# Forty of the first token block's expert sums moved from VectorE to GpSimd in a decoder layer kernel

## What is computed

```python
def peer_ffn(x, w_query, sub_keys, expert_u, expert_v):
    ...
    experts = jnp.take_along_axis(cand_idx..., top_pos, axis=-1)   # 128 experts for each token
    gate = jax.nn.softmax(top_s, axis=-1)
    def one_block(args):
        xb, eb, gb = args
        h = jax.nn.gelu(jnp.einsum('td,ted->te', xb, expert_u[eb]), approximate=False)
        return jnp.einsum('te,ted->td', gb * h, expert_v[eb])
    ...
h = layer_norm(ALPHA * h + ff, ln3_g[l], ln3_b[l])
```

## Time and profile before

| | us |
|---|---|
| median of 3 runs | 3145.84 |
| lowest and highest of them | 3145.17, 3148.16 |
| the profiled execution's own time | 3145.48 |
| its span | 3143.6 |

### The profile page before, as it was taken

How to read it: one execution, slowest core, us unless ns; L and a number is a source line. 1 busy time by engine, 2 the same in 40 slices (tenths; PEclk the granted TensorE clock), 3 DMA queues, 4 the chain that set the end, 5 groups by cost and what they waited for, 6 DMA issues and landing times. The chain is left out here.

```text
span 3143.6 us, 37681 instructions
## 1 busy us (share of the span) xinstructions
PE 2694.7 (86%) x16328; PEld 2218.2 (71%) x16328; DVE 1272.7 (40%) x1693; ACT 426.7 (14%) x916; POOL 803.9 (26%) x536
## 2 busy tenths in 40 slices
PE   8899999998999999999898986788766767676566
PEld 7898899998889899889898885788422223222222
DVE  0122001010100155734443455447677775655654
ACT  1121100021000111111101210101100001211121
POOL 0000000000000011212211232233466565555652
PEclk9999999999999999999999988899888888888899
DMA  8976378776837799998998989999999999999996
GB/s 326 305 267 227 136 296 298 285 296 228 311 138 287 260 363 385 354 369 344 424 424 357 383 321 423 420 396 425 409 421 422 421 421 421 421 422 421 422 422 280
DMA packets 126932, 1096.41 MB, mean 349 GB/s; under 512 B 13440, under 2 KB 22064, under 8 KB 28080
## 3 DMA queue, kind: packets, MB, share of 16 engines
q1 hardware_dynamic: 50512, 542.08, 44.3%
q0 software_dynamic: 76256, 551.94, 42.9%
HBM read 1084.52 MB, written 9.44 MB: 348 GB/s over the span
## 5 line engine op out<-in xcount | busy, mean ns | idle before, releaser
L601 PE MATMUL PS<-arena 128*128 128x128 f32 (+1 forms) x13952 | 1883.7, 297 | 78.4 <-DMA arena<-units 64.5
L601 PEld LDWEIGHTS PS<-arena 128*128 128x128 f32 x13952 | 1798.6, 194 | 158.5 <-DMA arena<-units 57.7
L949 PE MATMUL PS<-arena 128*128 128x512 f32 x1152 | 628.6, 706 | 275.8 <-DMA arena<-peer_v,arena 264.2
L949 PEld LDWEIGHTS PS<-arena 128*128 128x128 f32 x1152 | 254.1, 228 | 649.3 <-issue 591.8
L1382 DVE CUSTOM_DVE_ANT_0 arena<-arena 128x2048 f32<-128x2048 f32 x256 | 586.8, 2292 | 287.5 <-DMA arena<-peer_u,arena 281.0
L566 POOL DMA_INDIRECT arena<-peer_u,arena x256 | 399.1, 1559 | 892.5 <-DVE arena L1382 678.2
L566 POOL DMA_INDIRECT arena<-peer_v,arena x256 | 393.8, 1538 | 449.3 <-PE PS L949 214.2
L1392 DVE SCALAR_TENSOR_TENSOR arena<-arena 128x2048 f32<-128x2048 f32 x112 | 263.4, 2352 | 132.0 <-DMA arena<-peer_v,arena 128.7
L972 ACT ACTIVATE arena<-PS 128x512 f32<-128x512 f32 (+2 forms) x154 | 84.5, 549 | 1313.5 <-PE PS L601 1199.9
L1347 ACT ACTIVATE arena<-arena 128x128 f32<-128x128 f32 x144 | 57.9, 402 | 722.9 <-PE PS L949 721.5
L537 POOL DMA_DIRECT2D arena<-ln_rows x2 | 1.3, 640 | 384.7 <-DVE arena L1727 384.7
(11 more groups left out here) (186 smaller groups left out, 1049.0 us busy)
## 6 DMA issues: line engine op xcount, KB each, us to landing
arena<-units SPq DMA_DIRECT2D x243, 2048.0 KB, 9.1
arena<-w_ukv SPq DMA_DIRECT2D x16, 512.0 KB, 10.4
arena<-ln_rows SPq DMA_DIRECT2D x6, 1024.0 KB, 14.8
arena<-ln_rows POOLq DMA_DIRECT2D x4, 1024.0 KB, 18.6
arena<-peer_u,arena POOLq DMA_INDIRECT x256, 23.5
arena<-peer_v,arena POOLq DMA_INDIRECT x256, 23.8
rb_scratch<-arena POOLq DMA_DIRECT2D x1, 3072.0 KB, 38.5
arena<-rb_scratch SPq DMA_DIRECT2D x12, 256.0 KB, 9.8
```

The source lines that it names most:

```text
L601: ins = mm(bank[:, first:first + rhs.shape[1]], lhs, rhs, start=k == 0, stop=k == KT - 1)
L949: ins = mm(Y[c], diag[:, n % 4 * P:(n % 4 + 1) * P], rows[b][:, c * 512:(c + 1) * 512], start=n == first_used[tb], stop=False, skip_group_ ...
```

## The change

1. **More V rows early, and spread wider.** `SOON` goes from 28 to 40 and `FIRST` from 72 to 52: from U row 52 to U row 127, 40 V rows stand between them, about one behind every second U row. `LATE` becomes 168, the rest 344 entries.
2. **GpSimd sums them.** A new `add_row` on GpSimd scales the row in place by its gate and adds it to `acc`, two instructions over 128x2048 fp32. It stands in GpSimd's queue behind the fetch of the entry four places later (`LAG` = 4) and waits for its row to land. VectorE's own sums into `acc` wait until all 40 are there.
3. **Turns count dots only.** VectorE's turns hold 3 dots where they held 4 entries (scores aside). The turn in the second norm is gone. All 128 dots are done by the third step of CO.
4. **Gates earlier.** gelu and gates of the first `HALF` slots (40, were 56) are made between the recurrence and the branch gates. ScalarE's `gelu(0)` moves ahead of the gate evacuations.
5. **No identity matmuls.** `LAST` and L956 go; `last_norm` first adds each PSUM bank to VectorE's sums. VectorE and TensorE now alternate up to the last row.
6. In the last part `choose(1, k)` comes every six dots, not eight.

```diff
-HALF = 56
-FIRST = 72
-SOON = (NE - FIRST) // 2
+HALF = 40
+FIRST = 52
+SOON = 40
 GATED = 112
-LAST = 4
+LAG = 4
...
     for e in range(NE):
         order.append(("U", e))
-        if e >= FIRST and (e - FIRST) % 2:
-            order.append(("V", (e - FIRST) // 2))
+        if e >= FIRST and len(order) - e <= (e - FIRST + 1) * SOON // (NE - FIRST):
+            order.append(("V", len(order) - e - 1))
...
+                elif before[1] < SOON:
+                    pool.wait_ge(added, before[1] + 1)
...
-            for kind, s in ARRIVALS:
+            def add_row(s):
+
+                b, nth, _ = ROWS["V", s]
+                if s == 0:
+                    pool.wait_ge(begun, 1)
+                    pool.wait_ge(gated, 1)
+                else:
+                    pool.wait_ge(added, s)
+                pool.wait_ge(row_landed[b], 16 * (nth + 1))
+                nc.gpsimd.tensor_scalar(rows[b], rows[b], gates[0][:, s:s + 1], None, ALU.mult).then_inc(scaled_row, 1)
+                pool.wait_ge(scaled_row, s + 1)
+                nc.gpsimd.tensor_tensor(acc, acc, rows[b], ALU.add).then_inc(added, 1)
+
+            for n, (kind, s) in enumerate(ARRIVALS):
                 gather(kind, s)
+                if n >= LAG and ARRIVALS[n - LAG][0] == "V" and ARRIVALS[n - LAG][1] < SOON:
+                    add_row(ARRIVALS[n - LAG][1])
...
-                if e == NE - LAST:
-
-                    pe.wait_ge(v_summed, summed_to(s))
-                    for c in range(4):
-                        ins = mm(Y[c], ident, sums[tb][:, c * 512:(c + 1) * 512], start=False, stop=False, skip_group_check=True)
-                    ins.then_inc(all_summed, 1)
...
-                end = min(at[0] + n, LATE)
-                for kind, s in ARRIVALS[at[0]:end]:
-                    if kind == "U":
-                        dot(s)
-                    else:
-                        if s == 0:
-                            gate(0)
-                        add_row(s)
+                end = min(at[0] + n, NE)
+                for e in range(at[0], end):
+                    dot(e)
...
                 for s in range(8):
+                    if tb and s == 1:
+                        gate(0)
...
                 second_norm(tb)
-                if tb:
-                    turn(4)
                 choose(tb, 0)
...
-            def last_norm(tb, parts, done):
-
+            def last_norm(tb, banks, done):
+
+                parts = [sums[tb][:, c * 512:(c + 1) * 512] for c in range(4)]
                 for c in range(4):
+                    link(v.tensor_tensor(parts[c], parts[c], banks[c], ALU.add))
                     link(v.bn_stats(stats[:, 48 + 6 * c:54 + 6 * c], parts[c]))
```

More of the change, by code:

```diff
@@ L126, in on_vector @@
     if s < SOON:
-        return True
-    if s % NE >= NE - LAST:
         return False
@@ L138, in used_to @@
 def used_to(s):
-    return s + 1 - summed_to(s)
+    return s + 1 - SOON - summed_to(s)
 def arrivals():
@@ L394, in trunk_layer @@
         dot_done, gelu_done, v_summed, v_used = (sem(n) for n in ("dot_done", "gelu_done", "v_summed", "v_used"))
-        gated, all_summed = sem("gated"), sem("all_summed")
+        gated, begun, scaled_row, added = (sem(n) for n in ("gated", "begun", "scaled_row", "added"))
         gh_done, diag_done = sem("gh_done"), sem("diag_done")
@@ L1252, in trunk @@
                     mean_roots(q)
+                    gelu(0)
                 for j in range(4):
@@ L1269, in trunk @@
                             relu_out(tb, s)
-                if tb:
-                    gelu(0)
                 q_out(tb, 0)
@@ L1390, in add_row @@
                     dve.wait_ge(gh_done, e + 1)
+                elif summed_to(s) == 1:
+                    dve.wait_ge(added, SOON)
                 dve.wait_ge(row_landed[b], 16 * (nth + 1))
@@ L1690, in trunk @@
                 if tb:
-                    turn(4)
+                    turn(3)
                 gated_sums(q)
                 if tb:
-                    turn(4)
+                    turn(3)
                 normed_out(q)
                 if tb:
-                    turn(4)
+                    turn(3)
                 for s in range(8):
+                    if tb and s == 1:
+                        gate(0)
                     if s < 4 * (tb + 1):
@@ L1747, in trunk @@
                 second_norm(tb)
-                if tb:
-                    turn(4)
                 choose(tb, 0)
                 final_rows(tb)
-                link(v.tensor_scalar(sums[tb], h_tok[tb], ALPHA, None, ALU.mult))
+                mark(v.tensor_scalar(sums[tb], h_tok[tb], ALPHA, None, ALU.mult), begun, tb + 1)
             trunk(0)
@@ L1758, in _ @@
             trunk(1)
-            turn(LATE)
+            turn(NE)
             gate(1)
-            def last_norm(tb, parts, done):
+            def last_norm(tb, banks, done):
+                parts = [sums[tb][:, c * 512:(c + 1) * 512] for c in range(4)]
                 for c in range(4):
+                    link(v.tensor_tensor(parts[c], parts[c], banks[c], ALU.add))
                     link(v.bn_stats(stats[:, 48 + 6 * c:54 + 6 * c], parts[c]))
@@ L1780, in _ @@
                     dot(s)
-                    if s % 8 == 1 and s // 8 - NE // 8 < PEER_HEADS - 1:
-                        choose(1, s // 8 - NE // 8 + 1)
+                    k, more = divmod(s - NE, 6)
+                    if more == 1 and k < PEER_HEADS - 1:
+                        choose(1, k + 1)
                 else:
@@ L1786, in _ @@
                     if s == NE + PK:
-                        dve.wait_ge(all_summed, 1)
                         dve.wait_ge(v_used, used_to(NE - 1))
@@ L1791, in _ @@
                         add_row(s)
-            dve.wait_ge(all_summed, 2)
             dve.wait_ge(v_used, used_to(TB * NE - 1))
```

## The result

| | us |
|---|---|
| before, median | 3145.51 |
| after, median (lowest, highest) | 3237.89 (3235.54, 3238.32) |
| ratio, 95% interval | 1.0291, 1.0274 to 1.0309 |
| span of the profiled execution, before and after | 3143.6, 3236.5 |

The change costs 92 us. The forecast was 3151 with a range of 3116 to 3184.

A forecast was written before the change was run, and what follows sets the result against it. Total taken as transfers, which alone set the pace from 2220 us on, plus idle DMA time. 13.1 + 25.4 - 4.7 - 30.0 - 7.5 + 9 = +5.3 us on 3145.5 gave 3151, range 3116 to 3184.

The forecast's parts named there:

- Term 6: GpSimd's own passes over the early V rows: +9 us, from 0 to 39, for VectorE instructions that may find GpSimd at work.
- p: GpSimd's price per early V row, two passes: taken as 7 us, with bounds of 2.35 and 9.4 us.
- The second rival: GpSimd becomes the bound in attention turns and cross-attention heads, deciding from p = 7.3 us: slower, 3181, chance 0.20.
- Terms 1 to 3: Rows moved between stages of the first part: attention +13.1 us, merge to cross-attention +25.4, CO to PQ -4.7.
- Term 1: Attention: 13 more rows cost 32.5 us, less 19.4 us of idle DMA time, +13.1 us.
- the faster rival: The passes get their rows for free, 8.4 us idle at 1650 fills, GpSimd costs nothing: 3129, chance 0.23.
- Term 3: CO to PQ: 13 fewer rows; TensorE can't use the freed transfers, only its wait for the keys goes, -4.7 us.
- The gap: CO to PQ: DMA engines lack 13 rows, 32.5 us, before TensorE's last unit; later rows can't fill it.
- Term 4: Rows-only part: 12 rows fewer at 2.50 us each, -30.0 us.
- Term 5: The end, from the last landing to the last matmul and bank additions: -7.5 us.
- The third rival: GpSimd's first sum waits for late gates of slots 0 to 39, stalling all rows: time near no change, chance 0.04.
- The case at the faster end: The faster rival, 3129, chance 0.23; its floor, with all 25 early rows free, is 3108.

The follow-up runs named there:

- no sums: The changed kernel with GpSimd's two passes over each of the 40 early V rows replaced by one-column writes, sums left out: 3150.84 us, 1.0019 of before.
- four writes: The changed kernel with four GpSimd writes of the landed row's buffer in place of the two passes, sums left out: 3174.06 us, 1.0093.
- the long writes: The changed kernel with five GpSimd writes of the row's buffer and one of 1408 columns in place of the passes, sums left out: 3202.64 us, 1.0187.
- the run with VectorE's sums: The changed kernel with the 40 early sums done by VectorE in its turns, same order of rows: 3160.39 us, 1.0047.
- the new end alone: The kernel before without identity matmuls, V rows alternating up to the last, bank sums added by VectorE: 3139.49 us, 0.9981.
- the faster version: The kernel before with the new end, 34 early V rows instead of 28, summed by VectorE, four entries per attention turn instead of three: 3124.62 us, 0.9937.

## Why the prediction failed, and where it held

**Term 6, GpSimd itself, failed.** Said +9 us, from 0 to 39; it was +87 (from no sums to the changed kernel). Three things in it were wrong.

- *The price.* I put p at 7 us, with 9.4 as the upper bound, by VectorE's passes. It is 10.4. The bound took the dearer pass for two of VectorE's; the scaling, with one tensor input, takes 5.63 us, 2.4 of them, and is dearer than the addition. The sign given for a wrong forecast, over 3165 if p is over 8, came. The forecast itself said that the Trainium skill gives 4497 ns for the addition ("GPSIMD Engine Reference", "Performance versus the Vector engine"); the trace's shortest is 4493. Where no row showed the price, the bound from the nearest row should have been left much wider at the top, and the range with it.
- *The threshold.* I let the queue cost nothing up to p = 7.3. At 7.25 us, with writes that leave VectorE's instructions at their length, it cost 23 us (two runs, 9 us to either side), though GpSimd was still waiting 434.7 us for dots in that run. The budget was made per turn, as if fetches could be issued at any time in it. They can't: a buffer is set free by a dot, and a sum that GpSimd is busy with then delays the fetch, the row, and VectorE's next dot. Two waits show it. VectorE's for U rows grows from 357.2 us without sums to 408.2 with four writes and 473.2 with the long ones; TensorE's for the first norm from 19.7 to 34.2 and 40.8. (The 281.0 us before are no measure for this, for there VectorE also does the early sums.) How small a sum must be to cost nothing was not measured.
- *Exclusion.* The forecast cited the Trainium skill, "SBUF — State Buffer", "Who interferes with whom": a VectorE instruction with two SBUF inputs contends with a GpSimd instruction that reads SBUF and not with one that only writes. The trace agrees with both halves: an instruction with two SBUF inputs goes from 0.69 to 4.86 us and a dot to 6.50 while GpSimd reads, the statistics with one input stay at 0.69, and with GpSimd only writing all dots stay at 2292 ns. One instruction with a single tensor input grew too, the first norm's scaling, from 1.35 to 2.53 us. The sum took two and a half GpSimd passes, 9 us, for this; passes that read instead of writes were worth 35 us.

**The second rival was the mechanism**, GpSimd as the bound, and from the point given, p above 7.3, it was the right case. Its 3181 was 57 us short. Against the run without sums, GpSimd's part is 16 us by the last attention group, 57 by the first norm, 73 by the fourth head and 79 by the first fetch of the second part. The rival had 26 for the attention, where it took 16, and 12.5 for the heads, where it also took 16; what it left out is merge, mix and first norm, 41 us. The 35 us of exclusion are spread over these stages.

**Terms 1 to 3 came out in their sum, and that was luck.** They said +13.1, +25.4 and -4.7, together 33.8; without sums it was 40.0. By the table of stages it was -2.2 for the attention, +21.4 from there to the fourth head, and +20.8 behind it.

- *Term 1* was too dear: the idle transfers from 1650 to 1700 us, which it left out because of a wait of GpSimd, filled as well. Their share rose from 0.84 to 0.95 without sums, as the faster rival had it.
- *Term 3* had the wrong sign. It asked only whether TensorE could use free transfers, and took away a wait. But all of the last dots now stand ahead of the second norm in VectorE's queue, where 17 entries had stood behind its start, and TensorE waits 29.67 us for that norm. That GpSimd waits for V rows to land (123.6 us in all) can add to it, but need not be there: in the run with VectorE's sums GpSimd has no such wait, and this stretch is still 24.0 us longer than before, with a wait of 33.4 us for the second norm. How much the waits for landing cost stays open.

The gap itself came as described. GpSimd's wait was forecast at near 100 us; it is 84.8 without sums, 92.9 with VectorE's sums and 72.6 in the changed kernel, where the last early rows come later. The end of cross-attention was to come some 38 us later; it is 19 without sums and 92 in the changed kernel.

**Term 4** said -30.0. By the profiled executions, from the first fetch of the second part to the end it is 919.9 us with the new end alone and 888.8 without sums: 31 us for 12 rows, as forecast. In the changed kernel it is 898.8, 10 more; the last two early sums stand between the second part's first fetches. With the long writes in the same places it is 899.6.

**Term 5** said -7.5 and was -6.6.

**What was priced at nothing**: the choices every six dots, rightly. VectorE's relief of 66 us, nearly so: giving it the forty sums, 94 us, costs 10 us. The earlier gelu has no run of its own.

**The third rival**, sums that wait for late gates, did not come: GpSimd's first scaling starts at 1600.6 us, and the only waits ahead of its scalings are for rows to land, 23.2 us.

**The case at the faster end** did not come, but its idea was sound where it was applied with care: rows in idle stretches were free, and that is the faster version. The range's lower end was said to lie half of the way from 3129 to the floor of 3108, which is 3119 and not 3116; nothing hangs on it.

So the forecast was near in its sums (+3.8 us for the order, terms 1 to 4, against some 12 measured; -7.5 against -6.6 for the end), wrong in where the order costs its time, and far off in the one term that no row showed.

## What to carry to other kernels

Work given to the engine that issues the transfers also makes the transfers late, and not only when its queue is full: here forty pieces of 7.25 us cost 23 us although the queue still had idle time. Look too at what stands behind the late work in the next engine's queue: here it was a norm that TensorE waited for. Where transfers set the pace, lay the DMA share and the busy time of each stage beside a change that moves them: here moving a transfer out of a stretch that something else bounds and into a full one cost about its length (12 rows, 32 us), and filling idle stretches from a full one gained it (6 rows, 15 us). If a term rests on a duration that no row shows, measure that first, or widen the range.

## What the runs showed of the hardware

GpSimd's scaling of 128x2048 fp32 by a number per partition took 5.44 us at least, its addition of two such tiles 4.49, its write 1.81. On 1024 columns the two took 2.95 and 2.48 in the mean. The order of the first two was not expected.

An instruction of VectorE that stands behind a GpSimd pass is shown as busy, not as waiting: 4.86 us for 128x512 where it takes 0.69. The growth of the mean in the costliest groups (2292 to 2584 ns for the dots) is the sign.
